# Other counts of filling products ahead of two long TensorE loops, and half of a 64x64 turn made by the transposing form

## What is computed

```python
def _rwkv7_step(state, inp):
    r, w, k, v, kk, a = inp
    sa = jnp.einsum("dbhvk,dbhk->dbhv", state, kk)
    state = (state * w[..., None, :] - sa[..., None] * (kk * a)[..., None, :]
             + v[..., None] * k[..., None, :])
    return state, jnp.einsum("dbhvk,dbhk->dbhv", state, r)
...
_, y = lax.scan(_rwkv7_step, s0, (shared(r), to_scan(decay), to_scan(k_dir),
                                  shared(v), shared(kk), to_scan(iclr)))
```

## Time and profile before

| | us |
|---|---|
| median of 3 runs | 7332.48 (7325.83 to 7335.94) |
| the profiled execution | 7328.59 |
| its span, first to last instruction | 7326.6 |
| granted TensorE clock, mean | 0.907 |

### The profile page before, as it was taken

How to read it: one execution, slowest core, us unless ns; L and a number is a source line. 1 busy time by engine, 2 the same in 40 slices (tenths; PEclk the granted TensorE clock), 3 DMA queues, 4 the chain that set the end, 5 groups by cost and what they waited for, 6 DMA issues and landing times. The chain is left out here.

```text
span 7326.6 us, 207788 instructions
## 1 busy us (share of the span) xinstructions
PE 5876.2 (80%) x89758; PEld 4014.7 (55%) x89758; DVE 2999.9 (41%) x6257; ACT 2219.0 (30%) x3695; POOL 1907.7 (26%) x2010
## 2 busy tenths in 40 slices
PE   5999776776677789988888885797998777777778
PEld 4555665665566445545554553543545666666664
DVE  7001444544455233305544368313103454544551
ACT  3000344444344121213432232212002444444440
POOL 3550333333333135400001631000002333333330
PEclk8999888988889899998989897898998888889988
DMA  3221000000000222222112237421111000000002
GB/s 125 101 93 65 30 30 30 24 29 30 23 30 18 72 99 92 79 73 63 53 47 100 89 106 74 132 83 64 70 68 51 24 31 31 31 23 31 31 30 72
DMA packets 191740, 429.83 MB, mean 59 GB/s; under 512 B 23969, under 2 KB 107809, under 8 KB 190753
## 3 DMA queue, kind: packets, MB, share of 16 engines
q1 hardware_dynamic: 156000, 318.38, 14.7%
q10 hardware_dynamic: 34752, 96.51, 3.3%
HBM read 308.94 MB, written 105.87 MB: 57 GB/s over the span
## 5 line engine op out<-in xcount | busy, mean ns | idle before, releaser
L382 PE MATMUL ps<-arena 128*128 128x512 f32 x4544 | 1683.1, 532 | 55.0 <-ACT arena L336 18.4
L382 PEld LDWEIGHTS ps<-arena 128*128 128x128 f32 x4544 | 861.9, 190 | 871.9 <-issue 820.5
L1949 PE MATMUL ps<-arena 64*64 64x64 f32 x35840 | 846.8, 236 | 530.0 <-issue 469.4
L1949 PEld LDWEIGHTS ps<-arena 64*64 64x64 f32 x35840 | 728.2, 147 | 627.9 <-issue 624.6
L158 POOL TENSOR_TENSOR arena<-arena 128x512 f32<-128x512 f32 (+1 forms) x360 | 336.9, 953 | 1692.0 <-DMA arena<-w_mod 1681.7
L2317 ACT COPY arena<-ps 128x512 f32<-128x512 f32 (+1 forms) x880 | 541.1, 628 | 602.8 <-PE ps L1949 600.1
L2472 POOL TENSOR_TENSOR arena<-arena 128x256 f32<-128x256 f32 (+1 forms) x320 | 303.5, 950 | 1025.4 <-ACT arena L2321 366.4
L566 PE MATMUL ps<-arena 128*128 128x512 f32 (+1 forms) x1152 | 424.1, 528 | 18.2 <-ACT arena L336 18.2
L161 POOL TENSOR_TENSOR arena<-arena 128x256 f32<-128x256 f32 (+2 forms) x504 | 381.0, 768 | 52.0 <-issue 2.1
L1724 ACT COPY arena<-ps 128x1280 f32<-128x1280 f32 (+1 forms) x64 | 75.1, 1173 | 963.5 <-PE ps L382 749.0
L2392 POOL MEMSET arena<- 128x1280 f32 (+5 forms) x30 | 19.3, 698 | 1331.3 <-POOLq L88 1331.3
(11 more groups left out here) (268 smaller groups left out, 10872.9 us busy)
## 6 DMA issues: line engine op xcount, KB each, us to landing
arena<-proj SPq DMA_DIRECT2D x152, 640.0 KB, 5.0
proj<-arena ACTq DMA_DIRECT2D x80, 640.0 KB, 3.9
arena<-w_mod SPq DMA_DIRECT2D x96, 512.0 KB, 7.6
arena<-rw_w SPq DMA_DIRECT2D x68, 512.0 KB, 3.6
xres<-arena ACTq DMA_DIRECT2D x24, 640.0 KB, 7.0
arena<-na_w_in SPq DMA_DIRECT2D x24, 512.0 KB, 3.9
arena<-x SPq DMA_DIRECT2D x16, 640.0 KB, 7.2
arena<-xres SPq DMA_DIRECT2D x16, 640.0 KB, 6.9
```

Source lines behind the costliest of these rows:

```text
L382: last = nc.tensor.matmul(k.ps[:, 3 * u + n, 0:b - a], w[:, c * P:(c + 1) * P], src[:, c, a:b], start=(c == 0), stop=(c == KT - 1))
L1949: last = PE.matmul(part_of(out, dst, hh, g, d), part(l, src, hh, g, d), rhs, start=True, stop=True)
```

## The change

Three edits, all in the instructions of TensorE. The filling products become 79 and 70 instead of 70 and 69, with three plain increments behind those of the second layer. The call di becomes `turned`, which writes the same blocks in the same order, but for dst = 0 by `PE.transpose` (TensorE's transposing form, with the identity as moving operand) and only for dst = 1 by a product with the identity. `product` loses the branch for None. Waits and increments in the window stay as they are.

```diff
--- before.py
+++ after.py
@@ -1753,7 +1753,7 @@
 BACK = (0, 4, 3, 2, 1)
 
 
-LOOP_FILL = (70, 69)
+LOOP_FILL, LOOP_HOLDS = (79, 70), (0, 3)
 
 
 def rwkv_recur(nc, k, j, o, early):
@@ -1937,16 +1937,27 @@
                                                  ops[HP[hh], r, d, at:at + C], start=True, stop=True)
                 return last
 
-            def product(out, l, r, t):
-
+            def turned(out, m, t):
 
                 for d in range(2):
                     for g in range(2):
                         for hh in range(2):
                             for c in range(2):
                                 src, dst = c ^ (hh & t), c ^ (hh & (t + 1))
-                                rhs = k.eye2[HP[src], :] if r is None else part(r, src, hh, g, d)
-                                last = PE.matmul(part_of(out, dst, hh, g, d), part(l, src, hh, g, d), rhs, start=True, stop=True)
+                                to, of, eye = part_of(out, dst, hh, g, d), part(m, src, hh, g, d), k.eye2[HP[src], :]
+                                last = PE.matmul(to, of, eye, start=True, stop=True) if dst else PE.transpose(to, of, eye)
+                return last
+
+            def product(out, l, r, t):
+
+
+                for d in range(2):
+                    for g in range(2):
+                        for hh in range(2):
+                            for c in range(2):
+                                src, dst = c ^ (hh & t), c ^ (hh & (t + 1))
+                                last = PE.matmul(part_of(out, dst, hh, g, d), part(l, src, hh, g, d), part(r, src, hh, g, d),
+                                                 start=True, stop=True)
                 return last
 
             tiles = [(c, HP[c], hh, HP[hh]) for hh in range(2) for c in range(2)]
@@ -2061,7 +2072,7 @@
 
                 pe.wait_ge(f2_ev, it + 1)
                 hold(k, pe)
-                product(low[0], F, None, 3).then_inc(di_mm, 1)
+                turned(low[0], F, 3).then_inc(di_mm, 1)
 
                 states_seen(it, 1)
                 hold(k, pe)
@@ -2149,6 +2160,8 @@
             pe.wait_ge(zeroed, 1)
             for _ in range(LOOP_FILL[j]):
                 PE.matmul(bank[7][HP[0], 0:C], k.ident[HP[0], 0:C], k.ident[HP[0], 0:C], start=True, stop=True)
+            for _ in range(LOOP_HOLDS[j]):
+                hold(k, pe)
             with pe.Fori(0, KT) as e:
                 def lora_seen(i):
                     pe.wait_ge(lora_ev, e * 12 + (i + 1))
```

## The result

The changed kernel takes 7259.84 us (median of 4 runs, 7253.32 to 7264.28) against 7329.15 for the kernel before (4 runs, 7317.07 to 7335.94): a ratio of 0.9907, 95% interval 0.9889 to 0.9924. It is faster by 69 us, where 294 were forecast (7035 us). The time lies at the upper edge of the range given (7260). The sign was right and the size was not, by a factor of four.

What follows compares the result with a forecast made beforehand. The prediction took TensorE's instruction fetching, in blocks of 256, as the bound: 7328.6 - 335 (first loop kept) + 39 (transposes) + 2 (fill) = 7035 us, second loop's place at nothing; range 6900 to 7260.

Steps and rivals of the forecast that it cites:

- What bounds the kernel: Both recurrences: TensorE stalls at each new 256-instruction block; a window fetches nine blocks; 418 us of issue waits in the first.
- The store: TensorE's instruction memory: assumed to keep eight blocks, so the first loop, moved into seven plus one behind, is not refetched.
- The sharp edge: Both loops: seven blocks stay, eight (nine with the one behind) are fetched anew each turn.
- The gain in the first loop: First recurrence, 32 windows: 367 of stalls less 64 waited again plus 32 for clock, 335 us; ends 250 and 430.
- the waits that come due: First loop's local outputs and tail: waits hidden behind stalls, such as for VectorE, return; 2.0 x 32 = 64 us lost.
- the clock: First loop's windows: without standing still at the head the granted clock becomes 1.00; 1.0 us a window, 32 us gained.
- The transposes: Turned call: eight transposes replacing 16 passes cost +0.7 us a call, 39 us in all; ends 0 and +3.4 a call.
- The cover: Turned call in windows held by fetching: half its cost is hidden, 0.35 x 48 = 17 us.
- the small gain in place (109): Rival, first loop: still eight blocks, so it goes at the second loop's pace, 109 us less; total 7250; chance 8%.
- the rival: Fourth rival, turned call: transposes cost a high price, 272 us, for a time of 7494; chance not in the text.
- The fill and the second loop: Fill ahead of the loops: uncovered, 2 us together; second loop's place: still nine blocks, costed at nothing, ends -30 and +40.
- The signs: Profile after: q8 some 550 packets, kept windows 24 to 27 us, turned call 0.5 to 2; over 7150 blames waits due.

Runs made afterwards that it cites:

- both edits as measured alone: Two runs against the kernel before: only the filling-product counts changed (77, 62), 6950.52 us; only the transposes added, loop heads left where they were, 7593.85 us.
- the grouped call: Changed kernel with the turned call's same sixteen instructions reordered, first eight transposes, then eight products, loop heads unmoved: 6986.13 us, ratio 0.9516.
- the run with fewer: Kernel before with filling products cut from (70, 69) to (6, 5), loop heads at the same places inside a block: 7335.34 us, ratio 0.9986.
- the place alone: Kernel before with filling products (77, 62), no transposes: first loop's head at a block's beginning, in seven blocks, second loop unmoved: 6950.52 us, ratio 0.9489.

## Why the prediction failed, step by step

**What bounds the kernel**: right. The 836 packets, the stalls each 256 instructions and the difference between the two recurrences were the instruction stream; a count of small products that computes nothing of use moves the time by 378 us.

**The store**: right where it was used. A body that lies in seven blocks is kept; q8 fell to 548 packets, forecast "some 550". (That the store holds eight is the prediction's assumption. No packet comes in a kept window, not even for the block behind; whether that block is kept or not asked for, the runs don't tell.) The Trainium skill, "Runtime: NRT & Kernel Launch", section on instruction fetch, had two sentences: 2048 instructions for TensorE, and only two lines. These runs agree with the first and not, for this engine, with the second: 1791 instructions in a loop, and no packet in the middle windows. The sharp edge that the prediction took from it was too simple, but no step of the sum used it.

**The gain in the first loop**: 335 us forecast; 378 measured, the fill's change included. The term lies within its ends (250 and 430). The windows came to 24.7 us and not 25.5. Of its parts, the waits that come due were sized well (71 us more in the first recurrence, 64 set aside), and issue fell by 328 where 367 stood. The part that was too small is what TensorE gains in its own work: the forecast had 32 us for the clock, and the busy time of the same passes fell by 127. How much of that is the clock (0.89 to 0.97), and how much the passes no longer broken off by stalls, is not separated.

**The transposes**: this is the step that failed: "I take +0.7 us". In the changed kernel the term is 3.3 us a window by itself and 3.9 with the loop kept: 309 us where 39 stood. With both edits as measured alone the sum would be 7328.6 - 378 + 266 = 7217; the 43 us up to the 7260 measured are what the transposes cost more once the loop is kept. Three things were wrong in the term.

- *The row it was read from.* The prediction saw that each transpose stands alone between two products, and wrote down an upper end of +3.4 for it. It then went by the one change of form in the earlier trace rows, 0.20 us where 0.12 would be usual, as nearer the lower end. That row has one change; the call has 16, and what it pays is for each of them. The single records of the call show it, at full clock: a product starts 0.149 us behind the transpose, its second pass 0.107 behind that, and the next transpose 0.174 behind, 0.43 us for a pair that takes 0.10 in the grouped call. Even the excess of the row that was used, 0.08 us, times 16 gives 1.3 us and not 0.7.
- *The clock.* The term had none. With 16 changes the granted clock falls to 0.50 during or behind four calls in five, some 1.5 us a kept window on the mean. The prediction charged the clock to standing still only; in the window shown the engine is busy in every microsecond from the call's first pass to the clock's return, and what it did around the fall was 24 passes in 3.6 us.
- *The cover.* Half of the cost was to hide in the windows held by fetching. They rose by 2.8 to 3.7 us where the kept ones rose by 4.2, so no less than the call's own 2.7. TensorE's own time on the chain is added to the fetching, not hidden beneath it.

Its time, 7494, took the transposes' high price together with the small gain in place (109). The high price with the forecast's own gain, 7329 - 335 + 272 + 2 = 7268, was not written as a case, and is within 8 us of what came. That it is so near is in part luck: the gain was 43 us larger and the cost with the loop kept 37 us higher. The two terms hang together by some 43 us only, and should have been crossed. What the rival leaned on, the Trainium skill's "TensorEngine Tiling (Array Packing)", section on restrictions, says that column tiling disables the transposing form of float32. The runs agree with that as far as they go: the products here use half of the columns, and each change of form costs 0.13 to 0.21 us. They show the cost; that the exclusion is its reason was not tried.

**The fill and the second loop**: 2 us for the fill stands (0.108 us a pass, uncovered, and the run with fewer). The second loop's place was costed at nothing. The run with the place alone did not move that loop; in the grouped form, which did, its windows take 33.8 us for 33.0. The call is 0.3 of that (0.81 for 0.5), so what is left for the place is half a microsecond at most: in the range given.

**The signs** pointed at something, but not at the right term: with about 550 packets and a time over 7150 the text put the error on what comes due behind the stalls. That was the wrong place: with the place alone these waits grew by 71 us, about as forecast. The kept windows, 24 to 27 us in that list, came to 28.9, which doesn't say why. The right sign was another one in the same list, the duration of the turned call, "0.5 to 2 us", which came out as 3.3 to 4.4.

## What to carry to other kernels

Before changing TensorE's products in a loop, count the TensorE instructions of its body and where it stands in blocks of 256: place the head so that the body lies in as few blocks as it can, which here was worth 378 us for one loop of 1791 instructions (head at the beginning of a block) and 284 for the second (some 7 of them for the small products fewer, by the start of the first recurrence at 791 us for 798). Keep instructions of one form together: price a mixed sequence by the number of changes, not by the instructions, and look at the granted clock behind it. And where two terms of a sum are nearly independent, cross their ends, since the case that comes may be the one's middle with the other's end.

## What the runs showed of the hardware

- A loop whose TensorE instructions lie in seven blocks of 256 is not fetched again in its middle turns, with its last instruction at a block's very end too. With its end 3 and 35 instructions over, 1.0 and 4.0 packets come per middle window, at 0.9 to 1.3 us each; with 76, 92 and 103 over, all nine.
- Sixteen changes between the transposing form and half-width products, in float32 and 64x64, make a call of 24 passes take 3.26 us at full clock; the same passes with eight changes take 1.61 and with two 0.81.
- The granted clock fell to 0.50 within or just behind 64 of 80 calls with 16 changes, 6 of 80 with 8, and none of 80 with 2. In the one shown the engine was busy in every microsecond around the fall. All three orders have the same eight transposes in a call, so it goes with the order, not with the number of transposes. The Trainium skill, "TensorE: Matmul & The Clock Gate", "Part 4: PE-mode transpose", says that the full clock does not engage for the transposing form. In the grouped call eight transposes of 64x64 in a row ran at a granted 1.00; no run here has transposes alone for longer, so the sentence itself is not tried.
